# Decoder trunk: memory keys and values, token rows, first norm and split woven into one stage

## The reference

```python
def rmsnorm(x, g):
    return x * lax.rsqrt(jnp.mean(x * x, axis=-1, keepdims=True) + EPS) * g

mem_n = rmsnorm(mem_prompt, norm_mem)              # (256, 1024)
mk = (mem_n @ xa_wk).reshape(1, 256, 4, 256)       # output, and cross-attention's keys
mv = (mem_n @ xa_wv).reshape(1, 256, 4, 256)       # output, and its values
xn = rmsnorm(h, norm_mix_pre)                      # h = the 1056 token rows
proj = xn @ w_in                                   # the next stage begins with this
```

## Time and profile before

| | |
|---|---|
| median of 2 runs | 5146.7 us (5142.91 to 5150.49) |
| the profiled execution's own time | 5147.97 us |
| its span, from first to last instruction | 5146.2 us |
| mean granted TensorE clock | 0.939 of full |
| busy in the span | PE 4486.0 us (87%), DVE 2694.9 (52%), ACT 1510.4 (29%) |

### The profile page before, as it was taken

The page is one execution under the profiler, slowest core; times in us unless marked ns, Lnnn a source line. Parts: engine busy times, 40 slices in busy tenths (PEclk is TensorE's granted clock), DMA queues, the critical chain, the costliest instruction groups (busy, mean ns, idle before and its releaser), DMA issues. The chain is left out here.

```text
span 5146.2 us, 69476 instructions
## 1 busy us (share of the span) xinstructions
PE 4486.0 (87%) x28541; PEld 4095.5 (80%) x28541; DVE 2694.9 (52%) x4941; ACT 1510.4 (29%) x2249; POOL 235.9 (5%) x168
## 2 busy tenths in 40 slices
PE   5489999999899996787699999996998888999996
PEld 2479888889798886787588888885986878999995
DVE  1335455332388862697466776764553244443343
ACT  0212222221285542211144444443451251000001
POOL 0000000000011111211000000000001100000000
PEclk8799999989899998998799999998999898999998
DMA  3322222233355545455300000003222212111111
GB/s 117 97 67 81 80 78 76 63 101 112 118 137 154 147 122 135 130 159 181 112 19 18 18 18 18 20 12 128 80 97 82 77 59 66 42 42 42 42 33 68
DMA packets 360314, 417.73 MB, mean 81 GB/s; under 512 B 49082, under 2 KB 293740, under 8 KB 358876
## 3 DMA queue, kind: packets, MB, share of 16 engines
q1 hardware_dynamic: 347199, 368.00, 23.4%
q0 software_dynamic: 8192, 27.97, 2.0%
q10 hardware_dynamic: 4608, 17.30, 0.9%
HBM read 289.10 MB, written 121.77 MB: 80 GB/s over the span
## 5 line engine op out<-in xcount | busy, mean ns | idle before, releaser
L2215 PE MATMUL bank<-sum_x_hi,sum_w_hi 128*128 128x352 f32 x768 | 264.3, 344 | 112.4 <-DVE sum_x_lo L2198 41.9
L516 PE MATMUL bank<-xn_hi,pz_whi 128*128 128x352 f32 (+1 forms) x984 | 330.4, 336 | 20.2 <-DVE pz_wlo L501 14.6
L516 PE MATMUL bank<-xn_hi,pz_wlo 128*128 128x352 f32 (+1 forms) x984 | 321.5, 327 | 0.0
L516 PE MATMUL bank<-xn_lo,pz_whi 128*128 128x352 f32 (+1 forms) x984 | 320.1, 325 | 0.0
L3549 PE MATMUL bank<-bx_hi,bp_whi 128*128 128x384 f32 (+1 forms) x768 | 275.6, 359 | 33.1 <-DVE bx_lo L3607 19.9
L516 PE MATMUL bank<-xn_hi,pb_whi 128*128 128x352 f32 x816 | 275.3, 337 | 20.0 <-DVE pb_wlo L501 14.2
L180 PE MATMUL bank<-mlp_hidden_hi,mlp_wh 128*128 128x352 f32 x768 | 256.0, 333 | 36.5 <-DVEq L220 34.4
L530 ACT ACTIVATE ring<-bank 128x352 f32<-128x352 f32 (+1 forms) x273 | 125.6, 461 | 544.2 <-PE bank L516 543.9
L180 PE MATMUL bank<-bx_hi,mlp_wh 128*128 128x352 f32 x768 | 250.2, 326 | 29.6 <-DVE mlp_wl L195 21.5
L190 ACT ACTIVATE mlp_wh<-ring 128x2048 fp32r<-128x2048 f32 x32 | 61.2, 1914 | 704.9 <-PEq L183 696.4
L516 PE MATMUL bank<-xn_lo,pb_whi 128*128 128x352 f32 x816 | 265.9, 326 | 0.0
(11 more groups left out here) (684 smaller groups left out, 11789.2 us busy)
## 6 DMA issues: line engine op xcount, KB each, us to landing
ring<-in_w_in_dram SPq DMA_DIRECT2D x90, 512.0 KB, 4.6
proj_scratch<-ring SPq DMA_DIRECT2D x66, 528.0 KB, 3.1
ring<-in_mlp_w_dram SPq DMA_DIRECT2D x32, 1024.0 KB, 5.3
m_seg<-acum_scratch SPq DMA_DIRECT2D x32, 512.0 KB, 7.0
gates_scratch<-ring SPq DMA_DIRECT2D x24, 528.0 KB, 4.7
merged_scratch<-sum_gate ACTq DMA_DIRECT2D x24, 528.0 KB, 5.0
m_raw<-proj_scratch SPq DMA_DIRECT2D x24, 512.0 KB, 6.1
ring<-mamba_scratch SPq DMA_DIRECT2D x6, 1408.0 KB, 14.0
```

What stands on the lines that cost most here:

```text
L516: last = self.nc.tensor.matmul(ps[0:n, 0:m], w[:, q, 0:n], self.pair[x][:, q, t0:t0 + m], start=q == 0 and j == 0, stop=q == KD - 1 and j ...
L2215: last = self.nc.tensor.matmul(self.banks[e % n][:, 0:m], w[:, b % 2, q, :], self.pair[x][:, q, t0:t0 + m], start=q == 0 and i == 0, stop= ...
```

## The change

The nine blocks become one, `front`, with one release behind it. Two classes give the streams that `weave` orders on each engine.

`FrontTokens` takes x by tiles and chunks. A tile of 128 rows is loaded into one of four slots as soon as the slot is free, turned into bank 0 (first four channel groups, copied out by ACT) and bank 1 (the others, by DVE). Three chunks of 384, 384 and 288 tokens are normed each by itself in bank 2: a chunk starts once its three tiles (the last: two tiles and the sample) are out. DVE's product with rstd and gain goes to a small buffer by pairs of channel groups; ACT makes the high half of xn from it, DVE the low half. xnT is gone. Each chunk of hT is stored to h_scratch by itself.

`FrontMemory` does memory's work beside it, with banks 3 and 4 for transposes, 7 for the sums (ACT squares all 2048 columns of memT in one instruction, into the buffer that later holds the keys), 5 and 6 for the products. A product of 8 matmuls is cut in two halves of 4, between which other work of PE can stand. xa_wk is loaded at once, the halves of xa_wv when the products of the key halves are done (`product`). The arithmetic is the same; chunks of the norm are 384, 384, 288 instead of 352 each.

```diff
-def load_tokens(k, tag, src, sample, dst):
...
-def split_pair(k, tag, x, pair):
...
-def gemm_rows(k, tag, W, lhs, evac):
...
-def memory(k):
...
+class FrontTokens:
+    CHUNKS = ((0, 384), (384, 384), (768, 288))
...
+        self.rows, self.srow, self.hT = sb("rows", [P, 4, D]), sb("sample", [NS, D]), sb("hT", [P, KD, NT])
+        self.sq, self.rstd, self.tmp = sb("sq", [P, 2, 384]), sb("rstd", [P, 384]), sb("tmp", [P, 2, 2, 384])
+    def at(self, j):
+        return 12 + 3.2 * j + 11 * (j // 3)
+    def sync(self, sp):
+        for j in range(8):
+            yield self.at(j) - 10.5
+            if j >= 4:
+                sp.wait_ge(self.turned, 2 * (j - 3))
+            sp.dma_start(self.rows[:, j % 4, :], self.src[j * P:(j + 1) * P, :]).then_inc(self.in_[j % 4], 16)
+            if j == 7:
+                sp.dma_start(self.srow[:, :], self.sample).then_inc(self.s_in, 16)
+        for c, (t0, m) in enumerate(self.CHUNKS):
+            yield self.at(3 * c + 2) + 6
+            sp.wait_ge(self.off[0], min(3 * c + 3, 8) + (c == 2))
+            sp.wait_ge(self.off[1], min(3 * c + 3, 8))
+            sp.dma_start(self.k.h_dram[:, :, t0:t0 + m], self.hT[:, :, t0:t0 + m]).then_inc(self.stored, 16)
+        yield 1000
+        sp.wait_ge(self.stored, 48)
+    def tensor(self, pe):
+        transpose, bank = self.nc.tensor.transpose, self.k.bank
+        for j in range(8):
+            yield self.at(j)
+            pe.wait_ge(self.in_[j % 4], 16 * (j // 4 + 1))
+            for g in range(2):
+                if j:
+                    pe.wait_ge(self.off[g], j)
+                for q in range(4):
+                    last = transpose(bank[g][:, q * P:(q + 1) * P], self.rows[:, j % 4, (4 * g + q) * P:(4 * g + q + 1) * P], self.k.ident[:, :])
+                last.then_inc(self.turned, 1)
...
+    def move_scalar(self, act):
+        for j in range(8):
+            yield self.at(j) + 0.6
+            act.wait_ge(self.turned, 2 * j + 1)
+            self.nc.scalar.activation(self.hT[:, 0:4, j * P:(j + 1) * P], self.k.bank[0][:, :].rearrange("p (q t) -> p q t", q=4), ACT.Copy).then_inc(self.off[0], 1)
...
+    def norm_at(self, c):
+        return self.at(3 * c + 2) + 2.0
+    def scalar(self, act):
+        activation = self.nc.scalar.activation
+        for c, (t0, m) in enumerate(self.CHUNKS):
+            t = slice(t0, t0 + m)
+            for q in range(KD):
+                yield self.norm_at(c) + 0.9 * q
+                n = 8 * c + q
+                if q == 0:
+                    act.wait_ge(self.off[0], min(3 * c + 3, 8) + (c == 2))
+                    act.wait_ge(self.off[1], min(3 * c + 3, 8))
+                if n >= 2:
+                    act.wait_ge(self.summed, n - 1)
+                activation(self.sq[:, n % 2, 0:m], self.hT[:, q, t], ACT.Square).then_inc(self.squared, 1)
+            yield self.norm_at(c) + 9
+            act.wait_ge(self.summed, 8 * (c + 1))
+            if c:
+                act.wait_ge(self.normed, 4 * c)
+            activation(self.rstd[:, 0:m], self.k.bank[2][:, 0:m], ACT.Ln, bias=self.k.eps[:, 0:1], scale=1.0 / D)
+            act.drain()
+            activation(self.rstd[:, 0:m], self.rstd[:, 0:m], ACT.Exp, scale=-0.5).then_inc(self.rooted, 1)
+            for j in range(4):
+                yield self.norm_at(c) + 13 + 1.5 * j
+                act.wait_ge(self.normed, 4 * c + j + 1)
+                activation(self.pair[0][:, 2 * j:2 * j + 2, t], self.tmp[:, j % 2, :, 0:m], ACT.Copy).then_inc(self.n_hi, 1)
+    def sums(self, pe):
+        for c, (t0, m) in enumerate(self.CHUNKS):
+            for q in range(KD):
+                yield self.norm_at(c) + 0.9 * q + 0.6
+                pe.wait_ge(self.squared, 8 * c + q + 1)
+                if q == 0 and c:
+                    pe.wait_ge(self.rooted, c)
+                self.nc.tensor.matmul(self.k.bank[2][:, 0:m], self.k.ones[:, :], self.sq[:, q % 2, 0:m], start=q == 0, stop=q == KD - 1).then_inc(self.summed, 1)
+    def vector(self, dve):
+        gain = self.k.col["norm_mix_pre"]
+        for c, (t0, m) in enumerate(self.CHUNKS):
+            t = slice(t0, t0 + m)
+            for j in range(4):
+                yield self.norm_at(c) + 11.5 + 1.5 * j
+                if j == 0:
+                    dve.wait_ge(self.rooted, c + 1)
+                dve.drain()
...
+                last.then_inc(self.normed, 1)
+                yield self.norm_at(c) + 12.7 + 1.5 * j
+                if j:
+                    self.low(dve, c, j - 1, t, m)
+            yield self.norm_at(c) + 19
+            self.low(dve, c, 3, t, m)
...
+class FrontMemory:
...
+        self.rows, self.memT, self.keyT = sb("rows", [P, 2, D]), sb("memT", [P, KD, 256]), sb("keyT", [P, KD, 256])
+        self.made = [sb("key", [P, 2, D]), sb("val", [P, 2, D])]
+        self.sq, self.rstd = self.made[0][:, :, :].rearrange("p a n -> p (a n)"), sb("rstd", [P, 256])
+        self.raw = k.ring[:, :, :].rearrange("p s (t n) -> p s t n", t=KD)
+    LOAD = (5.0, 22.0, 40.0, 56.0)
+    START = (32.0, 48.0, 64.0, 80.0)
+    def sync(self, sp):
+        w, o = self.k.w, self.k.out
+        yield 0
+        for a in range(2):
+            sp.dma_start(self.rows[:, a, :], w["mem_prompt"][0][a * P:(a + 1) * P, :]).then_inc(self.in_, 16)
+        for n in range(4):
+            yield self.LOAD[n] if n < 2 else self.START[n - 1]
+            if n >= 2:
+                sp.wait_ge(self.product, 2 * (n - 1))
+            W = w["xa_wk" if n < 2 else "xa_wv"][0]
+            sp.dma_start(self.raw[:, n % 2, :, :], W[:, (n % 2) * 512:(n % 2 + 1) * 512].rearrange("(t p) n -> p t n", p=P)).then_inc(self.loaded[n % 2], 16)
+        for v, name in enumerate(("mem_k_prompt", "mem_v_prompt")):
+            yield (self.START[2], self.START[3] + 16)[v] + 2
+            sp.wait_ge(self.p_off, 4 * (v + 1))
+            sp.dma_start(o[name][0, 0].rearrange("(a p) h d -> p a (h d)", p=P), self.made[v][:, :, :]).then_inc(self.out, 16)
+        yield self.START[3] + 20
+        sp.wait_ge(self.k_off, 4)
+        sp.dma_start(self.k.key_dram, self.keyT[:, :, :]).then_inc(self.out, 16)
+        yield 1001
+        sp.wait_ge(self.out, 48)
+    def tensor(self, pe):
...
+        for n in range(4):
+            for a in range(2):
+                i = 2 * n + a
+                for half in range(2):
+                    yield self.START[n] + 7 * a + 3.5 * half
+                    if i == 0 and half == 0:
+                        pe.wait_ge(self.normed, 1)
+                    if half == 0:
+                        pe.wait_ge(self.loaded[n % 2], 16 * (n // 2 + 1))
+                        if i >= 2:
+                            pe.wait_ge(self.p_off, i - 1)
+                    for q in range(4 * half, 4 * half + 4):
+                        last = nc.tensor.matmul(bank[5 + i % 2][:, :], self.memT[:, q, a * P:(a + 1) * P], self.raw[:, n % 2, q, :], start=q == 0, stop=q == KD - 1)
+                last.then_inc(self.product, 1)
...
+    def products_vector(self, dve):
+        for i in range(8):
+            n, a = divmod(i, 2)
+            yield self.START[n] + 7 * a + 7.2
+            dve.wait_ge(self.product, i + 1)
+            self.nc.vector.tensor_copy(self.made[n // 2][:, a, (n % 2) * 512:(n % 2 + 1) * 512], self.k.bank[5 + i % 2][:, :]).then_inc(self.p_off, 1)
...
+    def scalar(self, act):
+        activation = self.nc.scalar.activation
+        yield 13
+        act.wait_ge(self.off, 4)
+        activation(self.sq, self.memT[:, :, :].rearrange("p t n -> p (t n)"), ACT.Square).then_inc(self.squared, 1)
...
+def front(k, pair):
+    w = k.w
+    with ExitStack() as ctx:
+        tokens = FrontTokens(k, ctx, w["x_prompt"][0], w["x_sample"].rearrange("b t d -> (b t) d"), pair)
+        memory = FrontMemory(k, ctx)
+        with k.nc.Block() as block:
+            @block.sync
+            def _(sp):
+                weave(memory.sync(sp), tokens.sync(sp))
+            @block.tensor
+            def _(pe):
+                weave(tokens.tensor(pe), tokens.sums(pe), memory.tensor(pe))
+            @block.scalar
+            def _(act):
+                weave(tokens.move_scalar(act), tokens.scalar(act), memory.scalar(act))
+            @block.vector
+            def _(dve):
+                weave(tokens.move_vector(dve), tokens.vector(dve), memory.vector(dve), memory.products_vector(dve))
+    release(k)
 def layer(k, ctx):
...
-    memory(k)
     with ExitStack() as s:
         pair = Pair(k, s, "xn")
-        with ExitStack() as s0:
-            xnT = act("xnT", s0)
-            with ExitStack() as s1:
-                hT = act("hT", s1)
-                load_tokens(k, "x", w["x_prompt"][0], w["x_sample"].rearrange("b t d -> (b t) d"), hT)
-                norm(k, "mixpre", hT, xnT, k.col["norm_mix_pre"], chunks3())
-                move(k, "h_out", k.h_dram, hT[:, :, :])
-            split_pair(k, "xn", xnT, pair)
-        release(k)
+        front(k, pair)
         project_and_mamba(k, pair)
```

(18 more changed lines are left out.)

146 lines of the change are left out of this document (86 added, 60 removed).

## The result

The kernel after took 5068.2 us (median of 2 runs, 5067.56 to 5068.76), before 5146.7: a ratio of 0.985, 95% interval 0.981 to 0.989. Two later series of five runs, each beside nine of before, gave 0.984 (0.982 to 0.986) and 0.982 (0.981 to 0.983). The prediction was 5068.0.

What follows compares the result with a forecast made beforehand. A chain through all engines bounded the kernel before; woven, PE should. 40.2 + 69.1 + 3.3 + 3.5 + 6.8 = 122.9 instead of 202.95, so 80.0 off 5147.97: 5068 us, range 5056 to 5088.

Steps and rivals of the forecast that it cites:

- The fill, first product at 40.2: Stretch 1, from the loads to the first product: loads, transposes, sums and table loads put that product at 40.2 us.
- The products' stretch, 72.4: Stretch 2, first to last product: 69.1 us of PE work plus 3.3 of waits, ending at 112.6.
- the small waits at the sums' two buffers: In the products' stretch: PE waits at the sums' two buffers, 1.5 us of the 3.3 of waits.
- Rival C: In the stage: orders of PE, ACT and DVE do not fit, PE waits 15 us instead of 3.3; 5080, chance 0.11.
- The tail, 10.3: Stretch 3, last product to w_in's issue: 3.5 us of last copies plus 6.8 from key_scratch's issue to the next stage.
- The h store, hidden: Beside the products: three h stores replace one of 11.8 us alone, 6.4 us per 384 tokens, and cost nothing.
- PE as the bound: In the woven stage: PE has the most work, some 83 us at full clock, and should set the end.
- the chain of chunk 2 that the prediction had named as late next: Ahead of product group 8: DVE's copy of group 6, queued behind chunk 2's work, is done some 5 us early.
- Rival B: In the fill: transfers share the queue, mem rows in at 32 instead of 15.3; 5085, chance 0.06.
- Rival D: Whole stage: the clock stays at its lower level, 1.2 GHz, 70.7 us more; 5139, chance 0.02.
- Rival E: In the queue: slow h stores hold up xa_wv; at 25 GB/s the stage ends near 238; 5183, chance 0.02.
- everything behind shifted by one constant within 2 us: Behind the stage: a sign to look for in the profile after, all later stages shifted equally, within 2 us.

Runs made afterwards that it cites:

- warm_fill: Kernel after plus four unread matmuls on PE in the idle 4.2 us ahead of chunk 0's sums; w_in issued at 119.08, whole run 5072.97 us.
- h_apart: Kernel after, but h stored whole in a block of its own behind the stage; w_in issued 10.9 us later, whole run 5091.65 us.
- few_values: Kernel after without 24 of the 32 matmuls of the value products; w_in issued at 108.85, whole run 5061.9 us.
- the halves alone: Two kernels, each weaving only tokens or only memory, the other part in before's blocks; w_in issued at 192.57 and 181.07 us, before 202.95.
- tokens_alone: Memory in the five blocks of the kernel before, then the new stage's token part alone; w_in issued at 192.57, 10.4 us earlier than before.
- the last experiment: Kernel after unchanged, and a combined version (extra matmuls, early keys, w_in and state rows loaded ahead), both rerun on one chip: 5059.3 and 5048.7 us.
- a_again: The kernel after, unchanged, timed again in turn with before; median 5066.3 us of 5 runs, ratio 0.984.
- a_third: The kernel after, unchanged, run once more on one chip with the combined version; 5059.3 us, ratio 0.982.
- keys_early: Kernel after, but keys transposed, copied and stored when made instead of behind the last value product; w_in issued at 119.72, 1.6 us earlier.
- prefetch: Kernel after with the 16 w_in loads issued inside the stage; first s5 product at 134.7 instead of 142.4, whole run 5071.1 us, ratio 0.983.

## Why the prediction was right

It was right in the whole, 5068.0 against 5068.2, and right in the mechanism: PE bounds the stage once the blocks are woven. That the numbers agree this closely is luck: the stage gave 81.6 us where 80.0 were said, with four terms off in both directions, the executions of after lie between 5054 and 5083 us in these series, and the parts behind took back 2.4 in the profiled one. Point by point:

- **The fill, first product at 40.2: it was 39.6.** Two terms were off against each other. Memory's sums took 3.6 us, not 5.0: the clock was at 1.00 in them. Chunk 0's took 8.4 instead of 7.1, inside the ends of 5.3 and 10.2. The prediction had the two levels and the place right, and mis-sized how long the lower one lasts. It took from the earlier trace rows three slow sums (3.8 us). Stretches of the kernel after:

```profile
30.25:37.00 6.75, 5.75 (x9) 3.05 (x10) 3.26 (x8) 3.14 (x8) 0.00 (x0) 0.50 0.65 259
37.25:39.63 2.38, 2.38 (x9) 1.08 (x8) 0.00 (x0) 1.88 (x4) 0.00 (x0) 1.00 0.00 0
```

  So the 0.65 over the sums is 0.50 for their first 5.75 us and 1.00 behind. `warm_fill` shows that the gap is the cause. The gap's length does not fix the price: `h_apart`, with the same gap of 4.22 us, was back at 1.00 at 34.9:

```profile
31.75:34.75 3.00, 3.00 (x6) 1.30 (x4) 2.42 (x7) 1.05 (x2) 0.00 (x0) 0.50 0.82 328
35.00:38.78 3.78, 3.78 (x11) 1.59 (x11) 0.00 (x0) 2.87 (x5) 0.00 (x0) 1.00 0.00 0
```

  The table loads are as in the earlier trace rows, here from ACT's timeline of the kernel after:

```profile
27.25 1.28 ACT L4216 ACT_TABLE_LOAD   x1
28.55 0.47 ACT L4216 ACTIVATE fm_rstd<-bank,eps 128x256 f32<-128x256 f32 x1
29.08 1.28 ACT L4218 ACT_TABLE_LOAD   x1
30.37 0.42 ACT L4218 ACTIVATE fm_rstd<-fm_rstd 128x256 f32<-128x256 f32 x1
30.69 0.92 ACT L4053 ACTIVATE ft_sq<-ft_hT 128x384 f32<-128x384 f32 x2
```

  The Trainium skill ("ScalarE: Activation LUTs", What ACT_TABLE_LOAD costs) has 2.66 us per switch. By that price, an estimate, the first square would have begun 2.8 us later than the 30.69 at which it did; here the row was the better guide.
- **The products' stretch, 72.4: it was 73.35.** The 64 products took their 54.9 us. Chunks 1 and 2 of the sums took 5.6 and 4.6 us and not 5.3 and 3.9, one us in all. Where two steps of 384 columns stood alone (54.47 to 55.76) they took 0.65 each, as priced; six in a row (59.20 to 63.53) took 0.72 each. This fits the small waits at the sums' two buffers, for which the prediction had 1.5 us among its waits, but the profile counts them as busy time, and no run takes them apart. The waits that it shows as idle time were 2.5 us, not 3.3: 1.17 where 1.8 were said, at tile 5's second group, behind DVE's copy, at the very place; 0.34 for an ACT copy; and 0.95 ahead of chunk 2's sums, which the prediction had not seen (the sample's transposes leave PE nothing else to do while ACT copies and squares). Rival C's 15 us did not come.
- **The tail, 10.3: it was 8.4.** This term was mis-sized the most. From the issue of key_scratch to the next stage took 5.0 us, not 6.8. In the transfers of before, that store landed after 5.9 us, with the two outputs of memory (4.0 and 6.2 us) in front of it in the queue; after, mem_k had been stored 33 us earlier, and key_scratch landed after 3.9. From its landing to the next stage it was about one us in both. The term was taken over from a place where three stores were in flight, and only two were left. The views of transfers, before and after:

```profile
key_scratch<-keyT SPq DMA_DIRECT2D x1, 1024.0 KB, 5.9
```

```profile
out_mem_v_prompt_dram<-fm_val SPq DMA_DIRECT2D x1, 1024.0 KB, 4.0
key_scratch<-fm_keyT SPq DMA_DIRECT2D x1, 1024.0 KB, 3.9
```

- **The h store, hidden: shown** by `h_apart` (12.4 us when it stands alone). **PE as the bound: shown** by `few_values` and by the halves alone; 8.1 us of the 20.6 were lost, most of them to the chain of chunk 2 that the prediction had named as late next. It had that copy some 5 us early, and it was 5.3.
- **Rival B:** mem rows were in at 15.2, as before; xa_wk landed after 14.3 us, not 10.3, behind the x tiles, and nobody waited for it. **Rival D:** the clock was 1.00 in the products' stretch. `tokens_alone`, at 0.65, comes near to what D described; with the products between the sums it did not come. The Trainium skill ("TensorE: Matmul & The Clock Gate", HAM oscillation) tells of a kernel that waits for a transfer behind each short group of matmuls and falls back to half rate each time. `tokens_alone` agrees, with waits for ACT and DVE in the transfer's place. **Rival E:** the stores of 1.5 MB landed after 6.7 us.
- **Wrong: "everything behind shifted by one constant within 2 us".** The gain against the first profile of before was 81.2 us at the first s5 product, 68.2 at the first product with pb, 76.2 at bp, 79.2 at the end. The code behind did not change, but the clock that it was granted did, as the last experiment shows for the stretch ahead of pb, where 13.4 us of the difference arose.

## What to carry to other kernels

Where a chain through all engines and a long product of PE stand one behind the other, weave them: the length comes to the busy time of the fullest engine, and the gain is more than each part gives alone (32 of 82 us here), because the gaps go and with them the halved clock. Of the 82 us the clock is the smaller part, 5. Price PE's work behind a gap of some us as a range between the two levels of the clock: the same gap of 4.22 us cost between 1.5 and 2.5 us here, by the sums' 7.4 to 8.4 us against 6.0 without it. Look at the place where the change ends, and not at the end of the program, when the difference is below some 15 us: identical code behind it spread by 17 us.

## What the hardware showed that was not expected

The gap of 4.22 us ahead of chunk 0's sums stands in seven profiles (`after`, `a_again`, `a_third`, `few_values`, `h_apart`, `keys_early`, `prefetch`). In each the granted clock fell from 1.00 to 0.50, but not at the same moment: in the kernel after at 30.2, one us before the sums began, and back at 37.0; in `h_apart` at 31.5, when they had begun, and back at 34.9. In the kernel before, behind the gap of 2.82 us that ends at 148.47, it was still 0.99 from 148 to 149 and then 0.50 from 149 to 152. A gap of 0.8 us (`warm_fill`) left it at 1.00.

And the clock also dips where PE is not idle at all: in the stretch of 344 to 358 us above it is 0.87 to 0.91 in the mean, and these ten us of it, in the kernel after, have PE busy for 10.00 us at 0.59:

```profile
1021.60:1031.60 10.00, 10.00 (x57) 10.00 (x56) 0.00 (x0) 0.08 (x1) 0.00 (x0) 0.59 0.00 0
```
